# Two one-tile subtractions in place of one two-tile subtraction on GpSimd, in an encoder that streams its weights

## The reference

```python
for layer in range(DEPTH):                      # DEPTH = 2
    h = rms_norm(x, mix_norm_g[layer])
    if layer % 2 == 0:
        x = x + conv_attention_mixer(h, ...)    # conv (31 taps) beside banded attention, then w_out
    else:
        x = x + short_conv_mixer(h, ...)        # bg, cg, u = h @ w_in; w_out(bg * conv3(cg * u))
    h = rms_norm(x, ffn_norm_g[layer])
    x = x + (jax.nn.silu(h @ w_gate[layer]) * (h @ w_up[layer])) @ w_down[layer]
```

## Time and profile before

| | |
|---|---|
| median of three runs | 2076.54 us (2074.66 to 2076.74) |
| profiled execution, device time | 2075.15 us |
| its span, first to last instruction | 2073.4 us |
| PE busy | 2056.8 us, 99% |
| PEld busy | 1715.7 us, 83% |
| DVE busy | 1465.4 us, 71% |
| ACT busy | 1111.6 us, 54% |
| POOL busy | 472.5 us, 23% |
| GpSimd's low parts (L633) | 159, together 390.2 us |
| GpSimd's tap sums (L645) | 96, together 83.1 us |

### The profile page before, as it was taken

One profiled execution on the slowest core, in us unless ns is written; L12 is line 12 of the kernel. 1 busy time (PEld: TensorE's weight loads), 2 busy tenths in 40 slices (PEclk: granted clock), 3 DMA queues, 4 the chain that ended last, 5 costly groups with the idle time before them and its releaser, 6 DMA issues.

```text
span 2073.4 us, 24352 instructions
## 1 busy us (share of the span) xinstructions
PE 2056.8 (99%) x9598; PEld 1715.7 (83%) x9598; DVE 1465.4 (71%) x1468; ACT 1111.6 (54%) x1265; POOL 472.5 (23%) x260
## 2 busy tenths in 40 slices
PE   9998999999999999999999999999999999999999
PEld 8888788888888888888888888888888888888887
DVE  5888889836887268864776784488638983489832
ACT  6687656544555445554654554456445554455542
POOL 3777530031001410014111114400130003300033
PEclk9999999999999999999999999999999999999999
DMA  7534365555654566545566555565465555655554
GB/s 256 174 120 134 125 212 185 189 194 202 226 210 156 189 208 232 198 154 185 190 213 223 155 190 183 188 228 203 160 236 179 186 185 191 234 182 183 197 190 161
DMA packets 208450, 394.30 MB, mean 190 GB/s; under 512 B 11344, under 2 KB 21968, under 8 KB 208336
## 3 DMA queue, kind: packets, MB, share of 16 engines
q1 hardware_dynamic: 207760, 392.21, 55.7%
q10 hardware_dynamic: 576, 0.53, 0.1%
HBM read 390.60 MB, written 2.10 MB: 189 GB/s over the span
## 4 chain that ended last, share of the span: by engine, by line
PE 91%; DVE 4%; ACT 1%; issue 1%; DMA 0%; DVEq 0%; ACTq 0%
PE pair L727 11%; PE pair L729 11%; PE pair L728 11%; PE pair L808 11%; PE pair L810 11%; PE pair L809 11%; PE pair L793 6%; PE pair L795 6%; PE pair L794 6%; PE tbank L823 2%; DVE w_lo L1712 1%; PE pair L747 1%; DVE pair L1869 1%; PE pair L748 1%; PE pair L749 1%
## 5 line engine op out<-in xcount | busy, mean ns | idle before, releaser
L1226 ACT ACTIVATE w_hi<-w_raw 128x1024 fp32r<-128x1024 f32 x584 | 615.3, 1059 | 598.4 <-PE pair L729 291.1
L1712 DVE TENSOR_TENSOR w_lo<-w_raw,w_hi 128x1024 fp32r<-128x1024 f32 x425 | 546.0, 1287 | 374.5 <-ACT w_hi L1226 374.3
L633 POOL TENSOR_TENSOR w_lo<-w_raw,w_hi 128x1024 fp32r<-128x1024 f32 x159 | 390.2, 2455 | 1569.8 <-ACT w_hi L1226 1569.8
L808 PE MATMUL pair<-w_hi,xT_hi 128*128 128x512 f32 x1040 | 404.7, 389 | 0.4 <-DVE w_lo L1712 0.4
L810 PE MATMUL pair<-w_hi,xT_lo 128*128 128x512 f32 x1040 | 404.7, 389 | 0.0
L809 PE MATMUL pair<-w_lo,xT_hi 128*128 128x512 f32 x1040 | 404.6, 389 | 0.0
L1226 ACT ACTIVATE w_hi<-s_raw 128x1536 fp32r<-128x1536 f32 x182 | 270.9, 1488 | 184.0 <-PE pair L810 124.8
L1712 DVE TENSOR_TENSOR w_lo<-s_raw,w_hi 128x1536 fp32r<-128x1536 f32 x182 | 318.3, 1760 | 63.1 <-ACT w_hi L1226 62.9
L727 PE MATMUL pair<-w_hi,yT_hi 128*128 128x512 f32 x704 | 274.8, 390 | 0.0
L729 PE MATMUL pair<-w_hi,yT_lo 128*128 128x512 f32 x704 | 274.1, 389 | 0.0
L728 PE MATMUL pair<-w_lo,yT_hi 128*128 128x512 f32 x704 | 273.8, 389 | 0.0
(11 more groups left out here) (198 smaller groups left out, 2550.3 us busy)
## 6 DMA issues: line engine op xcount, KB each, us to landing
w_raw<-in_w_down SPq DMA_DIRECT2D x176, 512.0 KB, 4.2
w_raw<-in_w_up SPq DMA_DIRECT2D x110, 512.0 KB, 6.1
w_raw<-in_w_gate SPq DMA_DIRECT2D x110, 512.0 KB, 3.6
w_raw<-in_sc_in SPq DMA_DIRECT2D x72, 512.0 KB, 4.3
s_raw<-in_w_gate SPq DMA_DIRECT2D x44, 768.0 KB, 8.1
s_raw<-in_w_up SPq DMA_DIRECT2D x44, 768.0 KB, 7.8
w_raw<-in_w_in SPq DMA_DIRECT2D x52, 512.0 KB, 4.4
w_raw<-in_w_out SPq DMA_DIRECT2D x32, 512.0 KB, 4.3
```

The source lines that it names most:

```text
L633: nc.gpsimd.tensor_tensor(w_lo[at], raw(o), w_hi[at].bitcast(F32), ALU.subtract).then_inc(w_lo_pool, 1)
L808: nc.tensor.matmul(b, x_hi(k, t), w_hi[:, r + kk, :], start=(first[t] and kk == 0), stop=False)
L1226: nc.scalar.activation(w_hi[:, tiles_of(o), :], raw(o), ACT.Copy).then_inc(w_hi_ready, 1)
L1712: nc.vector.tensor_tensor(w_lo[at], raw(o), w_hi[at].bitcast(F32), ALU.subtract).then_inc(w_lo_dve, 1)
```

## The change

GpSimd's low part of a slot is made by two instructions of one tile (512 elements per partition) in place of one of two tiles. Each raises `w_lo_pool` by one, so that whoever waits for a slot of GpSimd's waits for twice the count. Both tiles are still waited for together, by TensorE and by SP. VectorE's low parts keep one instruction.

```diff
         def low_done(engine, o):
 
-            engine.wait_ge(w_lo_pool if ON_POOL[o] else w_lo_dve, LOW_COUNT[o])
+            if ON_POOL[o]:
+                engine.wait_ge(w_lo_pool, SLOT_K * LOW_COUNT[o])
+            else:
+                engine.wait_ge(w_lo_dve, LOW_COUNT[o])
...
             def low(o):
 
-                at = (slice(None), tiles_of(o))
                 pool.wait_ge(w_hi_ready, o + 1)
-                nc.gpsimd.tensor_tensor(w_lo[at], raw(o), w_hi[at].bitcast(F32), ALU.subtract).then_inc(w_lo_pool, 1)
+                for kk in range(SLOT_K):
+                    at = (slice(None), TILE_AT[o] + kk)
+                    nc.gpsimd.tensor_tensor(w_lo[at], raw(o)[:, kk, :], w_hi[at].bitcast(F32),
+                                            ALU.subtract).then_inc(w_lo_pool, 1)
```

## The result

| | median | lowest and highest | runs |
|---|---|---|---|
| before | 2075.95 us | 2074.66 to 2081.27 | 12 |
| changed | 2080.8 us | 2076.25 to 2089.61 | 12 |

The ratio is 1.0024, with a 95% interval of 1.0014 to 1.0033. The changed kernel is slower, and it scatters: its 12 times spread over 13 us, where 11 of the 12 before lie within 2.1 us. The profiled execution is the slowest, 2089.61 us with a span of 2087.8 us, so its trace shows the loss at its largest.

The account below looks back on a forecast made before the run. TensorE is fully busy from 310 to 2060 us, so only the first 310 us can change. Losses 1.83 less gains 1.74 give +0.1 on 2075.15 us; with 1.39 for the runs' median, 2076.6 us, range 2073.6 to 2079.2.

Parts of the forecast that it names:

- The half at 1.29 us: GpSimd's low part of 512 elements, interpolated at 1.29 us; a whole low part then takes 2.54, 0.14 more.
- VectorE getting in between two halves: VectorE's waiting instruction gets in after half a low part, ending up to 1.1 us sooner; the second half ends later.
- the losses there: TensorE waits for late second halves: 0.52 us at slot 9, 0.19 at 77, 1.12 at 81; sum 1.83.
- The gains: VectorE sooner before three TensorE idle times: normed queries 0.51 us, softmax 0.51, slot 48 0.72; sum 1.74.
- Rival B: Halves cost about 2.0 us, three slots pay, 4.4 us slower: 2080.9 us; 0.08 with other ways to pay twice.
- At 121.44 a small step: VectorE step waiting 3.62 us through two tap sums and a low part; getting in between halves gives no gain.
- the rule from the other rows: When an instruction ends, the engine that has waited for the shared port goes first.
- the bound that it drew: The length of GpSimd's instruction is the longest time that VectorE can be shut out; low part 2.40 us.
- Rival A: Port not given up between halves: low parts 0.14 us longer, slot 81 loses 0.14, nothing won; 2076.7 us, chance 0.20.
- the stretch at half clock: Behind the 3.40 us idle time before 204.32: 3.3 us, expected to stay; if not granted, 1.65 us saved.
- B and other ways to pay twice: Chance 0.08 for slower outcomes, including halves of about 2.0 us paid at the three slots.

Follow-up runs that it names:

- x3: Changed kernel with only the low parts before slot 68 in two instructions, later ones whole; 2081.39 us, ratio 1.0019 to before.
- z3: Changed kernel plus one GpSimd wait, before slot 47's low part, for the third softmax step; 2079.15 us, ratio 1.0017 to before.
- x1_again: The identical changed kernel run once more for a second trace; 2079.11 us, ratio 1.0012 to before.
- y1_before_late: Kernel before, whole low parts, with four small GpSimd additions behind slot 33's low part; 2081.55 us, ratio 1.003 to before.
- y2_before_yield: Kernel before, whole low parts, with GpSimd waiting at three places for VectorE's softmax steps; 2071.66 us, ratio 0.9984 to before.
- z2: Changed kernel plus one GpSimd wait, among the tap sums ahead of slot 39, for the second softmax step; 2073.62 us, ratio 0.9991.
- y3: Changed kernel with GpSimd waiting at three places for VectorE's softmax steps; 2073.77 us, ratio 0.9988 to before.
- z1: Kernel before, whole low parts, three softmax waits plus waits for normed queries and VectorE's slot 48 low part; 2072.21 us, ratio 0.9981.

## Why the prediction was wrong

**What held, to a few hundredths.** The half at 1.29 us; VectorE getting in between two halves at slots 9, 77 and 81; and the losses there. Slot 9, changed kernel:

```profile
34.64 3.68 POOL L637 TENSOR_TENSOR w_lo<-w_raw,w_hi 128x512 fp32r<-128x512 f32 x2 [4.32 <-ACT w_hi L1231]
...
38.37 0.50 PE L732 MATMUL pair<-w_hi,xT_hi 128*128 128x512 f32 x1 [0.36 <-POOL w_lo L637]
```

0.36 + 0.16 = 0.52 us, as predicted. Slot 81 (1.21 + 0.16, less the 0.26 that it lost before) is 1.11 against 1.12; slot 77's first matmul starts 0.42 us after the one before it in place of 0.23, 0.19 as predicted. The gains came too: the idle times of 0.35, 0.94 and 0.72 us are gone from the changed trace. (The forecast took 0.72 us for slot 48; with the 0.16 us that a bracket leaves out it is 0.88, a small slip.) TensorE is full from 324 us on. Rival B, dear halves of 2.0 us, is refuted by the measured 1.29.

**The step that failed.** "At 121.44 a small step waits through both tap sums and the low part, 3.62 us. If it gets in between the halves, the two steps behind it wait for the second half: no gain." The row was seen, and priced at no gain and no loss. In the first trace it cost 4.1 us, and the same step of the third softmax, which had no term, another 5.6 us of idle time. Two things were missed.

First, the rule from the other rows, that the one who waits gets in at the next boundary, does not hold at this place, and cutting GpSimd's work finer gives it nothing. The prediction's own rows spoke against the bound that it drew, that one instruction of GpSimd is the longest time that VectorE can be shut out: 3.62 us against 2.41. The step was starved in all nine traces that have no wait of GpSimd at or before this place. Rival A had the right remark (VectorE had missed two boundaries), but asked only what the halves would lose in effect, not what a row that goes on longer would cost.

Second, the end of that row moves. GpSimd's low part behind the eight tap sums starts at 122.64 before and at 123.96 now, 1.32 us later, while the reduction starts 0.31 us earlier. Of the 1.32 us, 0.60 are there before the first of the predicted losses: slot 9's low part starts at 34.64 in place of 34.04. How much of that the change makes is open, since this start lies between 33.9 and 34.9 in the traces with early halves and between 34.0 and 34.4 in the others. Another 0.22 us come up to the low part of slot 33 (100.05 in place of 99.23), and 3 x 0.14 us from the three low parts of slots 33, 35 and 37. Then the effect multiplies:

- `top` ends at 126.51 in place of 125.06: 1.45 us, the 1.32 and about 0.14 for the row's last low part.
- By then slot 41's high part is ready, so `neg_top` waits for a half and `sink_d` for the next: 1.28 + 1.18 in place of 2 x 0.17 us, 2.1 us more.
- VectorE's low part of slot 38 then meets a tap sum: 1.72 in place of 1.22 us.

Together 4.1 us, which is 131.47 against 127.39, the end of slot 38's low part. In x3 and z3 it is the same (5.44 us of idle time); in x1_again `neg_top` took 0.17 us, and the idle time is 4.12.

**The second term that was missing** is the clock. The forecast let the stretch at half clock stay or go, and never let a new one come. In the first trace the two new ones are 17.1 us at half clock. Over all 13 traces, span minus idle time minus half of the time at half clock lies between 2057.7 and 2061.4 us, while the spans range from 2070.4 to 2087.8. So these two terms carry most of the scatter (the half-clock term counts some idle time twice, where the stretch begins within it):

| | TensorE idle | at half clock | span |
|---|---|---|---|
| before | 11.1 | 3.4 | 2073.4 |
| changed | 19.9 | 20.5 | 2087.8 |
| x1_again | 13.2 | 6.8 | 2077.2 |
| y1_before_late | 15.1 | 10.2 | 2079.3 |
| y2_before_yield | 9.4 | 3.4 | 2071.6 |

**The chances.** "B and other ways to pay twice: 0.08" is where this outcome sat. That B's 2080.9 us lies beside the measured 2080.8 is chance: its halves of 2.0 us did not come. Of the kernel before, one of the 12 runs took 2081.27 us, but among the three runs shown there was none such; a spread of three runs was taken for the kernel's.

**What stays open.** Why the step behind a softmax reduction can miss boundary after boundary, when nearly all other instructions of VectorE get in at the first (about 290 that had waited over 0.3 us, while the row went on, in the 13 traces). In the second softmax, with a reduction over 2048 elements, it was starved in all nine traces with no wait and for two boundaries in z2, where GpSimd's row had run for 17 to 22 us. It was not in y2, y3 and z1, where the row had run for 8 to 9 us. So the length of the reduction does not decide it alone. Nor does the length of the row: before the third softmax step, behind a reduction over 1024 elements, it was 8.4 us in every trace. There the step was starved in 2 of the 6 traces that have halves before slot 68 and no wait there. In z3 it missed one boundary (1.16 us), in the others none. A lock's inner state was not measured, and neither the row's length nor that of VectorE's wait was varied on its own. That the executions of the kernel before above 2082 us are starvations in its third softmax is a guess from their size: none of them was traced, and beside y2 and y3 the kernel before itself had none in 30.

## What to carry to other kernels

An instruction of VectorE that collides with GpSimd can be shut out not for one of GpSimd's instructions but for as long as GpSimd has work in a row, here for 5.38 and 6.75 us where the same step takes 0.17 us undisturbed. What has to be short is the row, not the instruction. Cutting it finer did not help. One semaphore wait of GpSimd, 0.51 us of standing still, brought the changed kernel from 1.0024 of the time before to 0.9991 (z2), and three of them brought the kernel before to 0.9984 (y2).

In a row that shows one instruction waiting much longer than its kind, ask first what ends the wait and whether the change moves that, even when the gain there is nil. And when a wait of TensorE is at stake, price the half clock behind it along with the wait.

## What the runs showed of the hardware

- VectorE beside a row of GpSimd's back-to-back instructions: usually let in at the first boundary (as at slots 9, 77 and 81), but behind two of the softmax reductions held off through 2 to 6 boundaries, for 3.6 to 6.75 us, by instructions of 0.73 to 2.4 us each, until the row broke off, in ten of eleven cases by 0.04 us or more. With a break of the row 8 to 9 us earlier, three of three were let in at the first. A memset of 0.07 us passed at the same time.
- TensorE's half clock came in stretches of 3.4, 6.8 and 10.2 us, each during or behind idle time of 3.4 to 5.95 us in one piece. Behind the same 3.40 us came 3.4 us in eight of the 13 traces, 6.8 in four, and none in one (z3).
- GpSimd's subtraction costs 1292 ns for 512 elements per partition and 2399 for 1024: about 0.18 us for each instruction and 2.16 ns for each element.
